# Output projections and keys in the two-matmul form, with the first gate unit's last two tiles taken at its end

## What is computed

```python
def pool_layer(x, mem, ...):                       # layer A
    ...
    x = x + jnp.concatenate([grouped, mem_out], axis=-1) @ w_out
    return x + swiglu(rmsnorm(x, norm_ffn), w_gu, w_down)

kv = rmsnorm(x, kv_norm) @ w_kv                    # keys and values of layer B, from A's result
k_sh = kv[..., :SB_WIDTH]; v_sh = kv[..., SB_WIDTH:]

def sb_layer(x, mem, k_sh, v_sh, ...):             # layer B
    ...
    x = x + jnp.concatenate([sb_out, mem_out], axis=-1) @ w_out
    return x + swiglu(rmsnorm(x, norm_ffn), w_gu, w_down)
```

## Time and profile before

| what | us |
|---|---|
| median of 3 runs | 891.33 (889.78 to 893.73) |
| the profiled execution, its device time | 892.28 |
| its span, first to last instruction | 890.2 |
| DVE busy | 671.9 |
| ACT busy | 483.4 |

### The profile page before, as it was taken

One profiled execution on the slowest core, in us unless ns is written; L12 is line 12 of the kernel. 1 busy time (PEld: TensorE's weight loads), 2 busy tenths in 40 slices (PEclk: granted clock), 3 DMA queues, 4 the chain that ended last, 5 costly groups with the idle time before them and its releaser, 6 DMA issues. The chain is left out here.

```text
span 890.2 us, 19346 instructions
## 1 busy us (share of the span) xinstructions
PE 872.7 (98%) x7632; PEld 793.1 (89%) x7632; DVE 671.9 (75%) x999; ACT 483.4 (54%) x779; POOL 115.3 (13%) x133
## 2 busy tenths in 40 slices
PE   7999999999999999999999999999999999999998
PEld 7998888888889988898888888899999888899998
DVE  6996887777677776868777767786996777747785
ACT  5674465555545566745555554458624554534453
POOL 2002300000022000050000006640008010000000
PEclk8999999999999999999999999999999999999999
DMA  9443455554557432254555445674534343244441
GB/s 339 176 162 121 154 184 188 186 186 144 171 190 250 149 136 98 93 190 160 182 183 184 175 151 184 203 261 159 180 131 132 122 130 79 95 141 143 167 166 48
DMA packets 23409, 144.48 MB, mean 162 GB/s; under 512 B 2968, under 2 KB 3224, under 8 KB 9648
## 3 DMA queue, kind: packets, MB, share of 16 engines
q1 hardware_dynamic: 22032, 140.26, 45.5%
q0 software_dynamic: 1168, 3.23, 1.6%
q10 hardware_dynamic: 144, 0.06, 0.0%
HBM read 142.47 MB, written 1.06 MB: 161 GB/s over the span
## 5 line engine op out<-in xcount | busy, mean ns | idle before, releaser
L2067 DVE TENSOR_TENSOR lo<-raw,hi 128x1024 fp32r<-128x1024 f32 (+1 forms) x210 | 243.9, 1203 | 12.2 <-ACT hi L1483 8.6
L580 PE MATMUL ps<-X,hi 128*128 128x512 f32 x704 | 249.0, 398 | 0.0
L579 PE MATMUL ps<-X,lo 128*128 128x256 f32 x704 | 198.4, 282 | 0.6 <-DVE X L2082 0.6
L573 PE MATMUL ps<-X,hi 128*128 128x256 f32 x600 | 174.1, 290 | 0.8 <-DVE X L2081 0.7
L574 PE MATMUL ps<-X,hi 128*128 128x256 f32 x600 | 169.7, 283 | 0.0
L575 PE MATMUL ps<-X,lo 128*128 128x256 f32 x600 | 169.6, 283 | 0.0
L580 PEld LDWEIGHTS ps<-X,hi 128*128 128x128 f32 x704 | 132.3, 188 | 32.7
L579 PEld LDWEIGHTS ps<-X,lo 128*128 128x128 f32 x704 | 133.0, 189 | 1.8 <-issue 1.2
L580 PE MATMUL ps<-H,hi 128*128 128x512 f32 x352 | 122.4, 392 | 0.0
L1483 ACT ACTIVATE hi<-raw 128x1024 fp32r<-128x1024 f32 (+1 forms) x109 | 107.7, 988 | 25.0 <-DMA raw<-in_down 13.6
L573 PEld LDWEIGHTS ps<-X,hi 128*128 128x128 f32 x600 | 114.8, 191 | 5.4 <-issue 3.9
(11 more groups left out here) (394 smaller groups left out, 1448.7 us busy)
## 6 DMA issues: line engine op xcount, KB each, us to landing
raw<-in_wide SPq DMA_DIRECT2D x106, 1024.0 KB, 4.9
raw<-in_down SPq DMA_DIRECT2D x32, 704.0 KB, 4.1
BI<-bias_table POOLq DMA_DIRECT2D x16, 128.0 KB, 4.8
raw<-in_wide SPq DMA_DIRECT2D x3, 512.0 KB, 9.0
X<-in_x SPq DMA_DIRECT2D x1, 1024.0 KB, 13.0
WG<-in_group SPq DMA_DIRECT2D x1, 768.0 KB, 17.1
out<-X SPq DMA_DIRECT2D x3, 256.0 KB, 2.4
cmask<-in_masks POOLq DMA_DIRECT2D x1, 544.0 KB, 5.9
```

The lines of the kernel that those rows point to most:

```text
L573: nc.tensor.matmul(dst, wh, xh, start=first, stop=False, skip_group_check=True)
L579: nc.tensor.matmul(bank[:, 0:T], wl, x[:, 0, :], start=first, stop=False, skip_group_check=True)
L580: return nc.tensor.matmul(bank, wh, x, start=False, stop=last, skip_group_check=True)
L2067: nc.vector.tensor_tensor(lo[:, s, a:b], raw[:, s, a:b], hi[:, s, a:b].bitcast(F32), ALU.subtract).then_inc(lo_ready, 1)
```

## The change

The output projections of layer A (four units), U_OUTB+2 and U_OUTB+3 of layer B and the three key units are computed with `wide_product`. They use the bank pairs by turns: A's gate units and down units are moved to other banks so that the turns go on. The halves are then added: for the projections DVE adds the left halves of both tiles in one instruction of 512 columns and then the right halves in the two instructions that were there. For the keys ACT first copies the right halves into KT (`k_lower_terms`), DVE adds the left halves to it and then multiplies. In the first gate unit of both layers the order becomes tiles 0 to 5 for m=0, 0 to 5 for m=1, 6 and 7 for m=0, 6 and 7 for m=1.

```diff
-        DOWN = OUTP
-        GATE_UP = (both, front)
+        DOWN = (PROJ, OUTP)
+        GATE_UP = ((front, both), (both, front))
+        K_BANKS = (both, front, both)
...
 # PE, unit_out
-                simple(HH, HL, 0, lambda u: mixed if u == U_OUTA else None)(u)
+                layer = 0 if u < U_GUA else 1
+                j = u - (U_OUTA, U_OUTB)[layer]
+                if layer == 1 and j < 2:
+                    return
+                if u == U_OUTA:
+                    pe.wait_ge(evac_done, first_group(u))
+                else:
+                    bank_free(first_group(u))
...
+                        last = wide_product(GATE_UP[layer][j % 2][:, m, :], hi[:, u % 4, c], lo[:, u % 4, c], H2[:, :, k, :],
+                                            k == 0, k == KD - 1)
 # PE, gu
-                    for m in range(2):
-                        half_ready(u, m)
-                        for k in range(KD):
+                    early_k = 6 if isinstance(u, int) and u == u0 else KD
+                    for k0, k1, m in ((0, early_k, 0), (0, early_k, 1), (early_k, KD, 0), (early_k, KD, 1)):
 # PE, unit_k
+                        last = wide_product(K_BANKS[j][:, m, :], hi[:, u % 4, c], lo[:, u % 4, c], X2[:, :, k, :], k == 0, k == KD - 1)
 # ACT
             def unit_qm(u):
                 if u == U_IN:
                     rstd(1, False)
+                else:
+                    k_lower_terms(2)
                 ahead(u)
+            def k_lower_terms(j):
+                act.wait_ge(unit_done, K_UNITS[j] + 1)
+                nc.scalar.activation(KT[:, 2 * j:2 * j + 2, :], K_BANKS[j][:, :, T:2 * T], ACT.Copy).then_inc(k_lower, 1)
+            def unit_k(u):
+                j = K_UNITS.index(u)
+                if j == 2:
+                    k_lower_terms(1)
+                ahead(u)
+                if j == 0:
+                    k_lower_terms(0)
 # DVE, unit_out
+                if layer == 0 or j > 1:
+                    banks = GATE_UP[layer][j % 2]
+                    x = X[:, 2 * j:2 * j + 2, :]
+                    nc.vector.tensor_tensor(x, x, banks[:, :, 0:T], ALU.add).then_inc(out_upper, 1)
+                    dve.wait_ge(out_upper, j + 1 if layer == 0 else 4 + j - 1)
+                    src = banks[:, :, T:2 * T]
 # DVE, unit_k
-                scaled(u, KT[:, 2 * j:2 * j + 2, :], 3)
+                keys_ = KT[:, 2 * j:2 * j + 2, :]
+                dve.wait_ge(k_lower, j + 1)
+                nc.vector.tensor_tensor(keys_, keys_, K_BANKS[j][:, :, 0:T], ALU.add).then_inc(evac_done, 1)
+                dve.wait_ge(evac_done, first_group(u) + 1)
+                dve.wait_ge(rs_done, 4)
+                nc.vector.tensor_tensor(keys_, keys_, twice(RS[:, 1, :]), ALU.mult)
+                ahead(u)
```

More of the change, by code:

```diff
@@ L279, in program @@
         lower_in = sem("lower_in")
+        k_lower, out_upper = sem("k_lower"), sem("out_upper")
         x_part = sem("x_part")
@@ L701, in mixed @@
                     pe.wait_ge(ml_ready, (k + 2, 1, 8)[max(0, k - 5)])
-                if U_OUTB <= u < U_OUTB + 2:
+                layer = 0 if u < U_GUA else 1
+                j = u - (U_OUTA, U_OUTB)[layer]
+                if layer == 1 and j < 2:
                     return
-                simple(HH, HL, 0, lambda u: mixed if u == U_OUTA else None)(u)
+                if u == U_OUTA:
+                    pe.wait_ge(evac_done, first_group(u))
+                else:
+                    bank_free(first_group(u))
+                if u == U_OUTA + 1:
+                    pe.wait_ge(att_out, 2)
+                    pe.wait_ge(grouped_free, 3)
+                if u == U_OUTB + 2:
+                    pe.wait_ge(sb_out, len(PAIRS))
+                for m in range(2):
+                    half_ready(u, m)
+                    for k in range(KD):
+                        if u == U_OUTA and m == 0:
+                            mixed(k)
+                        c = slice((m * KD + k) * P, (m * KD + k + 1) * P)
+                        last = wide_product(GATE_UP[layer][j % 2][:, m, :], hi[:, u % 4, c], lo[:, u % 4, c], H2[:, :, k, :],
+                                            k == 0, k == KD - 1)
+                last.then_inc(unit_done, 1)
             def half(u, n):
@@ L755, in unit @@
                     bank_free(u + (g0 - u0))
-                    for m in range(2):
-                        half_ready(u, m)
-                        for k in range(KD):
+                    early_k = 6 if isinstance(u, int) and u == u0 else KD
+                    for k0, k1, m in ((0, early_k, 0), (0, early_k, 1), (early_k, KD, 0), (early_k, KD, 1)):
+                        if k0 == 0:
+                            half_ready(u, m)
+                        for k in range(k0, k1):
                             if m == 0 and isinstance(u, int) and u == u0:
@@ L761, in unit @@
                             c = slice((m * KD + k) * P, (m * KD + k + 1) * P)
-                            last = wide_product(GATE_UP[(s - u0) % 2][:, m, :], hi[:, s, c], lo[:, s, c], X2[:, :, k, :],
+                            last = wide_product(GATE_UP[layer][(s - u0) % 2][:, m, :], hi[:, s, c], lo[:, s, c], X2[:, :, k, :],
                                                 k == 0, k == KD - 1)
@@ L792, in half @@
                         t = h * DN_TILES + k
-                        last = wide_product(DOWN[turn], hi[:, s, c], lo[:, s, c], H2[:, :, t, :],
+                        last = wide_product(DOWN[layer][turn], hi[:, s, c], lo[:, s, c], H2[:, :, t, :],
                                             h == 0 and k == 0, h == 1 and k == DN_TILES - 1)
@@ L803, in down @@
                         half(i * 4 + (u0 + j), (u0 + j) % 4)
-            def first_k(u):
-                return from_x(16) if u == U_K else None
+            def unit_k(u):
+                j = K_UNITS.index(u)
+                ready = from_x(16)
+                bank_free(first_group(u))
+                for m in range(2):
+                    half_ready(u, m)
+                    for k in range(KD):
+                        if j == 0 and m == 0:
+                            ready(k)
+                        c = slice((m * KD + k) * P, (m * KD + k + 1) * P)
+                        last = wide_product(K_BANKS[j][:, m, :], hi[:, u % 4, c], lo[:, u % 4, c], X2[:, :, k, :], k == 0, k == KD - 1)
+                last.then_inc(unit_done, 1)
             def operands(g):
@@ L1461, in _ @@
                 "gu": gu, "down": down,
-                "unit_k": simple(XH, XL, 0, first_k),
+                "unit_k": unit_k,
                 "logits": logits, "turn": turn, "pv": pv, "grouped": grouped,
@@ L1597, in lower_terms @@
                     act.wait_ge(unit_done, u + 1)
-                    nc.scalar.activation(GU[:, s % 2, :, :], GATE_UP[(s - u0) % 2][:, :, T:2 * T],
+                    nc.scalar.activation(GU[:, s % 2, :, :], GATE_UP[layer][(s - u0) % 2][:, :, T:2 * T],
                                          ACT.Copy).then_inc(lower_in, 1)
@@ L2045, in _ @@
                 "unit_qm": unit_qm, "unit_out": unit_out, "gu": gu, "down": down,
-                "unit_k": ahead, "esplit": esplit,
+                "unit_k": unit_k, "esplit": esplit,
                 "soft": soft, "norm": norm, "turn": turn, "pv": pv, "grouped": grouped,
@@ L2230, in unit_out @@
                 dve.wait_ge(unit_done, u + 1)
-                src = bank_of(u).rearrange("p (a b) -> p a b", a=2)
+                if layer == 0 or j > 1:
[4 more added lines that the diff above has]
+                    src = banks[:, :, T:2 * T]
+                else:
+                    src = bank_of(u).rearrange("p (a b) -> p a b", a=2)
                 nc.vector.tensor_tensor(X[:, 2 * j, :], X[:, 2 * j, :], src[:, 0, :], ALU.add).then_inc(x_done, 1)
@@ L2257, in hidden_in @@
                     dve.wait_ge(lower_in, u + (1 + m0 - u0))
-                    banks = GATE_UP[(s - u0) % 2]
+                    banks = GATE_UP[layer][(s - u0) % 2]
                     nc.vector.tensor_tensor(GU[:, s % 2, :, :], GU[:, s % 2, :, :], banks[:, :, 0:T],
@@ L2307, in half @@
                         dve.wait_ge(unit_done, u + 1)
-                        upper, lower_ = (DOWN[turn][:, n * T:(n + 1) * T].rearrange("p (a b) -> p a b", a=1) for n in range(2))
+                        upper, lower_ = (DOWN[layer][turn][:, n * T:(n + 1) * T].rearrange("p (a b) -> p a b", a=1) for n in range(2))
                         nc.vector.tensor_tensor(tile(X, m), tile(X, m), upper, ALU.add).then_inc(x_part, 1)
```

## The result

The changed kernel takes 893.26 us (median of 13 runs, 891.12 to 896.32) against 891.15 us (13 runs, 887.29 to 895.03) for the kernel before. The ratio of the two sets of runs is 1.0033, 95% interval 1.0017 to 1.005 (the quotient of the two medians is 1.0024): slower, by less than the 0.43% forecast. The profiled execution of the changed kernel took 896.05 us, span 894.0, beside 892.28 and 890.2 before.

The account below looks back on a forecast made before the run. PE sets the time, but DVE has little room and its added work stops PE. Losses of 1.3 + 1.4 + 1.0 = 3.7, rounded to 3.8 us, take the median from 891.33 to 895.1 us, 0.43% slower; range 890.0 to 898.0.

Parts of the forecast that it names:

- three stops of PE: PE waits ahead of the third gate unit in layers A and B and at M0: +1.3, +1.0, +1.4 us.
- the band from 893.5 to 896.8: Whole kernel: range of median times in us given to the main forecast, chance 0.55.
- The extra add: DVE's new 512-column add into X in projection units: 0.73 us each, between 0.41 and 0.85.
- Layer A: Projections to third gate unit: DVE's add 1.65 us late, so PE starts that unit 1.3 us later.
- Keys: DVE waits 2.5 us for ACT's copy at K1; lower parts come late and M0 ends 1.4 us later.
- Layer B: From U_OUTB+2 on: DVE 1.3 us late at the first gate unit's add, third gate unit 1.0 us later.
- The slack of 0.3 us: Ahead of the third gate unit in both layers: DVE's bank-freeing add could be some 0.3 us late without delaying PE.
- The cost of a product: On PE: 0.353 us two-matmul against 0.360 three-matmul, weight loads hidden; about 1.0 us gained over 9 units.
- The first rival: PE alone decides: 2.4 us gain, 888.9; with the keys' 1.4 standing, 891 to 892; chance 0.18 (PE alone or keys only).
- All that PE gained from the order is spent waiting: Layer A's third gate unit: the new order's gain, up to 0.7 us, is lost waiting for DVE's add.
- The sum of the three stages: Layer A, keys and layer B together: 1.3 + 1.4 + 1.0 = 3.7 us slower, rounded up to 3.8.
- recorded durations promised 27 us: Rival that weight loads count: 191 ns saved per product, 144 products, 27 us, giving 864; chance 0.02.

Follow-up runs that it names:

- the keys undone: Changed kernel with key units K0 to K2 back in the three-matmul form; ratio to the kernel before 1.0047 (6 runs), then 1.0037 (12 runs).
- What pays: Kernel before plus two-matmul keys (split first, K1 in other banks), new first-gate-unit order and its bank freed early; 889.81 us, ratio 0.9983.

## Why the prediction was right

It forecast 0.43% slower, by three stops of PE; it is 0.33% slower (0.17 to 0.5), and the three stops are there. The median, 893.26 us, lies 0.24 us below the band from 893.5 to 896.8 that had the chance of 0.55, so what bears the prediction out is the three distances more than the time.

- **The extra add**, taken as 0.73 us from L2259, lasts 0.67 to 0.69 and is 0.71 to 0.73 from its start to the next. Shown by leaving it out.
- **Layer A**, forecast +1.3: +1.16. The chain was as described, 1.4 us late at the bank's add instead of 1.65, since PE was done earlier than I had reckoned. The wait for POOL came too and lay inside, as the text had it.
- **Keys**, forecast +1.4: +1.36. DVE idle 2.54 us (forecast 2.5), M0's eighth product 22.9 us behind K0's first (310.03 - 287.17), as forecast (307.4 - 284.49). Shown by the split put first.
- **Layer B**, forecast +1.0: +1.00.
- **The slack of 0.3 us** ahead of the third gate unit: 0.30 us of wait appears and 0.25 of 0.7 is gained with the order alone; 0.71 once the bank is freed early.
- **The cost of a product** is the term that was mis-sized. 0.353 us was taken as the price of the two-matmul form; it is one of two. In the projections the products came at 0.347, so the four units of A took 22.32 us instead of 23.13, a gain of 0.81 where 0.41 was reckoned. The weight loads are hidden, as said: 64 loads fewer in A (192 before, 128 after) and a gain of 0.81 is 13 ns each, far from 191. With 0.40 in B (the part ahead of the first gate unit: 11.61 before, 11.21 after) and 0.30 at the keys the form is worth 1.5 us, not 1.0.
- **The first rival's price with the keys** was added up wrongly: of the gain of 2.4 the keys' 0.3 is already in their 1.4, so 891.33 - 2.1 + 1.4 makes 890.6, not 891 to 892.
- **"All that PE gained from the order is spent waiting"** was wrong for the changed kernel. I took the old order's waits to be contained in the wait for the bank, and didn't see that PE, stopped for longer, would be granted half its clock.

The sum of the three stages is 3.52 us (forecast 3.7), and profile against profile the time went from 892.28 to 896.05. 3.52 us would be a ratio of 1.0040, which lies inside the interval; the measured 1.0033 is about 2.9 us, and the two medians differ by 2.11. That the two profiled executions differ by what was forecast is in part luck: outside the three stages their stretches differ by up to 2 us either way, and the executions of one kernel spread over 7.7 us before and 5.2 us after.

## What to carry to other kernels

Price an instruction on a pipelined engine by the distance of starts; recorded durations promised 27 us here and the form was worth about 1.5. When work is moved from the engine that sets the time to the one that feeds it, follow the feeder's queue to the next thing that the first engine waits for: 0.73 us a unit on DVE came out as 1.16 and 1.00 us in the two layers, because almost nothing idle stood between. And look for what can be taken out of such a chain without moving it to another engine: putting one split and one bank-freeing add ahead of a wait brought the three stages down by 3.42 us.

## What the runs showed of the hardware

**Two paces of the same matmuls.** In long stretches without a wait the products of `wide_product` come 0.3467 or 0.3533 us apart on average, nothing between. At the faster pace every distance is 0.345 to 0.348 us, at the slower one they repeat by threes (about 0.346, 0.359 and 0.355). The pace changes where the stream is broken, by a wait or by other matmuls: in the kernel before the products from 99.50 to 101.93 come at 0.347, and from 103.49 on at 0.353, with the sum of squares and no listed wait of PE between. In three records, the changed kernel's among them, it also changed halfway through K0, where PE waits for nothing. Groups of instructions of the changed kernel, windows 120 to 130 and 440 to 450:

```profile
L583 PE MATMUL ps<-X,hi 128*128 128x512 f32 x30 | 10.6, 399 | 0.0
```

```profile
L583 PE MATMUL ps<-X,hi 128*128 128x512 f32 x30 | 10.4, 391 | 0.0
```

At a granted clock of 1.00 in both, the 512-column matmul is recorded as 399 or 391 ns. Over the 320 products of a gate stretch that is 2.1 us (111.0 or 113.1), over a down stretch 1.1 (62.6 or 63.7). In the eleven records gate A fell three times into the fast pace and gate B six times; the two records of one program (the keys undone) differ in three of four stretches. So it isn't fixed by the program. What picks it, and whether a kernel can make one likelier, stays open; it is enough for differences of several us between executions of one kernel, and with a few runs it can hide or feign an effect of the size studied here.

**The clock.** With the old order in the changed kernel PE was granted 0.50 over the whole window of 3.20 us shown there, behind a stretch in which it was busy for 1.01 of 1.90 us; at no single wait of up to 1.4 us in these stages did it fall. Executions differ in the same clock at their beginning, where the first unit still waits for its data. Windows of the changed kernel and of the second run with the keys undone:

```profile
10.00:14.00 4.00, 2.88 (x14) 2.62 (x14) 4.00 (x7) 3.50 (x7) 1.69 (x2) 0.50 1.03 415
```

```profile
10.00:14.00 4.00, 2.54 (x19) 2.31 (x19) 4.00 (x7) 3.37 (x7) 1.56 (x2) 1.00 1.04 405
```

With the same program up to there, one was granted half the clock and the other all of it, and their projections began at 73.13 and 71.22 us. In the eleven records that start lies between 70.78 and 73.50, another 2.7 us that have nothing to do with any edit, and they go with the clock: its mean from 5 to 20 us is 1.00 in the four records that start at 70.78 to 71.22, 0.89 in two (72.27 and 72.34) and 0.77 in five (72.78 to 73.50). How long PE waited there doesn't tell them apart: the second run with the keys undone waited 1.40 and 1.44 us and was granted 1.00 from 10 to 14, the kernel of "What pays" waited 1.42 and 1.44 us and was granted 0.57. The Trainium skill, "TensorE: Matmul & The Clock Gate", section "The HAM clock gate", describes a gate that follows PE's activity; the records agree in that the clock takes one of two levels and fell only after idle time.
